# Weight blocks of 128 columns at a pitch of 528 bytes instead of 512 in a partition, in a two-layer decoder kernel

## The reference

```python
def swiglu(h, wg, wu, wd):
    return (jax.nn.silu(h @ wg) * (h @ wu)) @ wd
...
for layer in range(DEPTH):
    h = rms_norm(x, ffn_norm[layer, 0])
    x = x + 0.5 * swiglu(h, ffn_w_gate[layer, 0], ffn_w_up[layer, 0], ffn_w_down[layer, 0])
    h = rms_norm(x, mix_norm[layer])
    if layer % 2 == 0:
        x = x + hybrid_mixer(h, ...)   # attention with three branches, and a short convolution
    else:
        x = x + pool_mixer(h, ...)     # means over windows of 2, 4, 8, 16 tokens, then 256x256 matrices
    h = rms_norm(x, ffn_norm[layer, 1])
    x = x + 0.5 * swiglu(h, ffn_w_gate[layer, 1], ffn_w_up[layer, 1], ffn_w_down[layer, 1])
```

## Time and profile before

| | |
|---|---|
| time of the runs | 1798.89 us median of 3 (1797.44 to 1799.77) |
| the profiled execution | 1798.12 us, of which the span from first to last instruction is 1796.3 us |
| PE busy | 1775.5 us, 99% of the span |
| DVE, ACT, POOL busy | 859.3, 598.6, 92.5 us |
| TensorE clock granted | 1.000 of full speed over the whole span |
| DMA | 163.68 MB, 91 GB/s over the span |
| share of PE in the chain that ended last | 95% |

### The profile page before, as it was taken

How to read it: one execution, slowest core, us unless ns; L and a number is a source line. 1 busy time by engine, 2 the same in 40 slices (tenths; PEclk the granted TensorE clock), 3 DMA queues, 4 the chain that set the end, 5 groups by cost and what they waited for, 6 DMA issues and landing times.

```text
span 1796.3 us, 22196 instructions
## 1 busy us (share of the span) xinstructions
PE 1775.5 (99%) x8164; PEld 1465.8 (82%) x8164; DVE 859.3 (48%) x1104; ACT 598.6 (33%) x838; POOL 92.5 (5%) x81
## 2 busy tenths in 40 slices
PE   8999999999999999999999999999999999999999
PEld 6888888877777878888888888888888888888887
DVE  5544443356788845444443344444432564444322
ACT  5333332235336534333222233232222533332211
POOL 0500000012000011000000000000000000000000
PEclk9999999999999999999999999999999999999999
DMA  6333343324320013333343323333432233333331
GB/s 177 94 93 99 99 115 97 89 75 104 83 82 13 1 47 94 96 102 93 93 125 96 95 82 94 102 96 93 124 97 66 77 94 98 101 93 107 113 96 47
DMA packets 321362, 163.68 MB, mean 91 GB/s; under 512 B 13893, under 2 KB 320041, under 8 KB 321322
## 3 DMA queue, kind: packets, MB, share of 16 engines
q1 hardware_dynamic: 321130, 163.08, 31.5%
q10 hardware_dynamic: 192, 0.08, 0.0%
HBM read 161.04 MB, written 2.10 MB: 91 GB/s over the span
## 4 chain that ended last, share of the span: by engine, by line
PE 95%; DVE 3%; ACT 1%; issue 1%; DMA 0%; SPq 0%; POOL 0%; ACTq 0%; DVEq 0%
PE ps_s L532 20%; PE ps_s L534 20%; PE ps_s L533 20%; PE ps_y L532 9%; PE ps_y L533 9%; PE ps_y L534 9%; PE ps_aux L867 2%; PE ps_y L850 1%; DVE w_lo L1407 1%; PE ps_s L818 1%; PE ps_aux L864 1%; ACT w_hi L1019 1%; PE ps_s L819 0%; PE ps_aux L869 0%; DMA x_in<-in_x 0%
## 5 line engine op out<-in xcount | busy, mean ns | idle before, releaser
L1407 DVE TENSOR_TENSOR w_lo<-raw,w_hi 128x1024 fp32r<-128x1024 f32 (+2 forms) x279 | 368.0, 1319 | 726.4 <-ACT w_hi L1019 725.9
L532 PE MATMUL ps_s<-xg_hi,w_hi 128*128 128x512 f32 x1576 | 618.8, 393 | 0.1
L534 PE MATMUL ps_s<-xg_hi,w_lo 128*128 128x512 f32 x1576 | 613.3, 389 | 0.0
L533 PE MATMUL ps_s<-xg_lo,w_hi 128*128 128x512 f32 x1576 | 613.3, 389 | 0.0
L1019 ACT CAST w_hi<-raw 128x1024 fp32r<-128x1024 f32 (+2 forms) x279 | 312.1, 1119 | 591.9 <-PE ps_s L534 298.1
L532 PEld LDWEIGHTS ps_s<-xg_hi,w_hi 128*128 128x128 f32 x1576 | 295.8, 188 | 65.8 <-issue 2.9
L533 PEld LDWEIGHTS ps_s<-xg_lo,w_hi 128*128 128x128 f32 x1576 | 295.9, 188 | 63.5 <-issue 2.4
L534 PEld LDWEIGHTS ps_s<-xg_hi,w_lo 128*128 128x128 f32 x1576 | 295.8, 188 | 61.9
L532 PE MATMUL ps_y<-act_hi,w_hi 128*128 128x512 f32 x704 | 274.3, 390 | 0.7 <-DVE w_lo L1407 0.7
L534 PE MATMUL ps_y<-act_hi,w_lo 128*128 128x512 f32 x704 | 273.9, 389 | 0.0
L533 PE MATMUL ps_y<-act_lo,w_hi 128*128 128x512 f32 x704 | 273.9, 389 | 0.0
(11 more groups left out here) (314 smaller groups left out, 1078.5 us busy)
## 6 DMA issues: line engine op xcount, KB each, us to landing
raw<-in_ffn_w_gate SPq DMA_DIRECT2D x88, 512.0 KB, 3.9
raw<-in_ffn_w_up SPq DMA_DIRECT2D x88, 512.0 KB, 3.9
raw<-in_ffn_w_down SPq DMA_DIRECT2D x64, 704.0 KB, 4.5
raw<-in_hyb_w_in SPq DMA_DIRECT2D x19, 512.0 KB, 3.8
x_in<-in_x SPq DMA_DIRECT2D x8, 256.0 KB, 6.0
raw<-in_hyb_cmp_w SPq DMA_DIRECT2D x4, 512.0 KB, 4.0
raw<-in_hyb_w_in SPq DMA_DIRECT2D x8, 256.0 KB, 3.3
raw<-in_hyb_w_out SPq DMA_DIRECT2D x16, 128.0 KB, 2.8
```

What stands on the lines that cost most here:

```text
L532: mm(bank, hi, x_hi, start=first, stop=False, **kw)
L533: mm(bank, hi, x_lo, start=False, stop=False, **kw)
L534: return mm(bank, lo, x_hi, start=False, stop=last, **kw)
L1407: tt(w_lo[:, n % 2, 0:size], raw[:, n % 4, 0:size], f32(w_hi[:, n % 2, 0:size]), ALU.subtract).then_inc(lo_ready, 1)
```

## The change

Both weight tensors get a fourth dimension. A block of 128 columns (512 bytes) is followed by 4 unused columns (16 bytes), so blocks stand 528 bytes apart; a slot of 11 blocks grows from 5632 to 5808 bytes, and each tensor by 352 bytes. `w_hi` keeps its position and `w_lo` moves by 352 bytes. The tensors behind `w_lo`, up to `token`, move by 704 bytes; `token` shrinks by 192 bytes (its unused part), so that everything behind it (`act_hi` and all later ones) moves by 512 bytes. `raw` keeps its layout. The cast of ACT and the subtraction of DVE cover the same elements with one more dimension in their access patterns. The order and the number of instructions on every engine are as before.

```diff
@@
 TE = T + 16
 PW = 2 * TE
+WP = P + 4
@@
         raw = sb("raw", [P, 4, KH2 * P])
-        w_hi = sb("w_hi", [P, 2, KH2 * P], F32R)
-        w_lo = sb("w_lo", [P, 2, KH2 * P], F32R)
+        w_hi = sb("w_hi", [P, 2, KH2, WP], F32R)
+        w_lo = sb("w_lo", [P, 2, KH2, WP], F32R)
@@
-        token = sb("token", [P, 80])
+        token = sb("token", [P, 32])
@@
+        def raw_blocks(n):
+
+            return raw[:, n % 4, 0:BLOCKS[n] * P].rearrange("p (k f) -> p k f", f=P)
@@
-                    last_mm = three(bank, w_hi[:, n % 2, k * P:(k + 1) * P], w_lo[:, n % 2, k * P:(k + 1) * P],
+                    last_mm = three(bank, w_hi[:, n % 2, k, 0:P], w_lo[:, n % 2, k, 0:P],
                                     tile_of(x_hi, k0 + k), tile_of(x_lo, k0 + k),
                                     first and k == 0, last and k == BLOCKS[n] - 1)
@@
-                w_h, w_l = (w[:, n % 2, k * 2 * P:(k + 1) * 2 * P] for w in (w_hi, w_lo))
+                w_h, w_l = (w[:, n % 2, 2 * k:2 * k + 2, 0:P] for w in (w_hi, w_lo))
@@
-                copy(w_hi[:, n % 2, 0:BLOCKS[n] * P], raw[:, n % 4, 0:BLOCKS[n] * P]).then_inc(hi_ready, 1)
+                copy(w_hi[:, n % 2, 0:BLOCKS[n], 0:P], raw_blocks(n)).then_inc(hi_ready, 1)
@@
-                size = BLOCKS[n] * P
-                tt(w_lo[:, n % 2, 0:size], raw[:, n % 4, 0:size], f32(w_hi[:, n % 2, 0:size]),
+                size = BLOCKS[n]
+                tt(w_lo[:, n % 2, 0:size, 0:P], raw_blocks(n), f32(w_hi[:, n % 2, 0:size, 0:P]),
                    ALU.subtract).then_inc(lo_ready, 1)
```

More of the change, by code:

```diff
@@ L554, in first_unit @@
                             turn_x(q, (KD - 1,))
-                    hi, lo = (w[:, 0, k * P:(k + 1) * P] for w in (w_hi, w_lo))
+                    hi, lo = (w[:, 0, k, 0:P] for w in (w_hi, w_lo))
                     pe.wait_ge(xg_hi_ready, place + 1)
@@ L613, in block_of @@
                 def block_of(m, k):
-                    return three(ps_s[:, 2 * m, :], w_hi[:, (n + m) % 2, k * P:(k + 1) * P],
-                                 w_lo[:, (n + m) % 2, k * P:(k + 1) * P], tile_of(xg_hi, k), tile_of(xg_lo, k), k == 0, k == KD - 1)
+                    return three(ps_s[:, 2 * m, :], w_hi[:, (n + m) % 2, k, 0:P],
+                                 w_lo[:, (n + m) % 2, k, 0:P], tile_of(xg_hi, k), tile_of(xg_lo, k), k == 0, k == KD - 1)
                 for k in range(KD // 2):
@@ L737, in compress @@
                         last_mm = three(ps_s[:, p % 4, 0:8 * NCP],
-                                        w_hi[:, n % 2, k * P:(k + 1) * P], w_lo[:, n % 2, k * P:(k + 1) * P],
+                                        w_hi[:, n % 2, k, 0:P], w_lo[:, n % 2, k, 0:P],
                                         b_hi, b_lo, h == 0 and k == 0, h == 1 and k == KD - 1)
@@ L907, in from_conv @@
                 for k in range(4, KD):
-                    three(ps_s[:, 2 + d % 2, :], w_hi[:, n % 2, k * P:(k + 1) * P], w_lo[:, n % 2, k * P:(k + 1) * P],
+                    three(ps_s[:, 2 + d % 2, :], w_hi[:, n % 2, k, 0:P], w_lo[:, n % 2, k, 0:P],
                           tile_of(ob_hi, k - 4), tile_of(ob_lo, k - 4), k == 4, False)
@@ L913, in from_attention @@
                 for k in range(4):
-                    last_mm = three(ps_s[:, 2 + d % 2, :], w_hi[:, n % 2, k * P:(k + 1) * P],
-                                    w_lo[:, n % 2, k * P:(k + 1) * P],
+                    last_mm = three(ps_s[:, 2 + d % 2, :], w_hi[:, n % 2, k, 0:P],
+                                    w_lo[:, n % 2, k, 0:P],
                                     tile_of(o_hi, k), tile_of(o_lo, k), False, k == 3)
```

## The result

The changed kernel takes 1830.64 us (median of 4 runs, 1830.29 to 1831.51) against 1798.62 us for the kernel before (also 4 runs), a ratio of 1.018 with a 95% interval of 1.0164 to 1.0196. Its profiled execution has a span of 1829.7 us, 33.4 more than before.

A forecast was written before the change was run, and what follows sets the result against it. The prediction took PE's matmul pace to bound the kernel. Offsets added +36 us, all other terms 0, which on the median of 1798.89 us gave 1835 us, with an 8 in 10 range of 1762 to 1848 us.

The forecast's parts named there:

- part 1: All 6840 matmuls with xg and act: new weight offsets lose the settled 226.7 ns pace for 232.0, +36 us.
- The upper bound, 233.3 ns for all: All 6840 matmuls run at the pace of the matmuls with o, +46 us.
- part 2: Some 190 256-column matmuls, 1.3 us either way, and 96 output-projection matmuls with o, already slow; taken as 0.
- part 3: ACT's cast and DVE's subtraction with one more dimension: at least nothing, at most a start per block; taken as 0.
- The upper bound of 1.4 us more: In DVE's subtraction, seven more starts of 203 ns each, one per block, 1.4 us; as much assumed for ACT.
- The helping rival: Spreading weight blocks removes a collision with the moving tile, so matmuls speed up: between 1753 and 1795 us, chance 0.29.
- The rival of no change: The matmul surcharge hangs on the moving tile's position, or 16 bytes don't matter: 1799 us, chance 0.12.

The follow-up runs named there:

- const64: Kernel before the change with all weight blocks at the pitch of 512 bytes but moved together by 64 bytes; 1841.77 us, ratio 1.0241.
- const16: Kernel before the change with all weight blocks at the pitch of 512 bytes but moved together by 16 bytes; 1840.79 us, ratio 1.0237.
- The map: Matmul-only kernels of their own, writing zeros: weight blocks at constant, then jumping offsets to the tile; constant offset 0 gave 226.6 ns, 32 gave 233.1.
- lo_only: Kernel before the change with the pitch of 528 bytes in w_lo alone, w_hi at 512 and offset 0; 1816.09 us, ratio 1.01.
- aligned: Kernel before the change with gaps bringing ones_r, o_hi, o_lo and pt_b to offset 0 modulo 256 too; 1797.72 us, ratio 0.9999.
- const240: Kernel before the change with all weight blocks at pitch 512, moved to offset 240 modulo 256 from the tiles; 1799.91 us, ratio 1.0011.

## Why the prediction was right

**The bound.** PE's pace was the only thing that moved: 33.1 us more of busy PE in 33.4 us more of span.

**Offsets, part 1.** The term was +36 us, by 232.0 - 226.7 = 5.3 ns on 6840 matmuls. Measured: 231.5 and 232.0 ns, 33.9 us by the starts, 32.0 by the medians. The pace borrowed from the ten matmuls of the earlier trace rows fits the changed kernel to half a nanosecond. The 4 us by which the term is too high are no more than the rounding of its rows: a row is rounded to 0.01 us, so ten matmuls give the pace only to 1 ns. The next use of `ones_r` in the trace of the kernel before has the same ten:

```profile
1055.48 0.39 PE L545 MATMUL ps_stat<-ss_parts,ones_r 128*128 128x512 f32 x1
...
1057.79 0.39 PE L534 MATMUL ps_s<-xg_hi,w_lo 128*128 128x512 f32 x1
```

These are 231.0 ns each, and the unrounded starts give 231.1 to 231.2 in all three places without a stop, which would have made the term 31 us and the time 1830. That the number fits so closely is in part luck in either case. The earlier trace rows average two matmuls at offset 96 and eight that recover at offset 0, while the changed kernel walks over offsets that, held constant, cost between 0 and 7.5 ns. The upper bound, 233.3 ns for all, is what `const64` and `const16` reach at 1841.8 and 1840.8 us: a constant bad offset is worse than the walk, since the walk passes the good ones too.

What I gave as the reason needs mending in two places. I said that the fast pace was seen only where the offset stays at 0 from one load to the next. The map shows a period of 256 bytes and further offsets that hold the fast pace, and bring it back after some stretches and not after others. And the jump is not what hurts. A pitch of 768 jumps by 256 bytes with every block and stays at 226.7. What counts is that loads stand at a bad offset modulo 256, even one in three of them (`lo_only`), and what ran before.

**256-column matmuls and `o`, part 2.** Taken as 0. In the changed kernel `o` lost some of its surcharge (233.3 before, 230.0 to 233.6 after), on 96 matmuls under 0.3 us. The pool mixer's stretch of the earlier trace rows went from 119.6 to 118.2 ns by the unrounded starts, and the compression's last two from 118.0 and 118.7 to 122.7; each comes to under 0.3 us.

**ACT and DVE, part 3.** Taken as 0; 1049 and 1243 ns measured. The extra dimension costs 5 ns on DVE and nothing on ACT. The upper bound of 1.4 us more is far off.

**The helping rival** fell: no constant offset of 32, no low block elsewhere and no pitch was faster than 226.6 ns. The compression's 113.2 ns, which spoke for it, did not carry over to tiles of 512. Its own two stretches do get slower at offset 0 (`aligned`), so for those 256-column matmuls an offset other than 0 is the faster one; whether that comes from the short run read four times no run shows. **The rival of no change** falls with `const16` and `const64`, in which only the weights stand elsewhere (all other tensors keep their places modulo 512). With it goes the price of 0 that the prediction drew from the page "SBUF — State Buffer" of the Trainium skill, section "Who interferes with whom": there PE has two independent read ports and never waits on anyone, while here the same matmuls take 226.7 or 233.3 ns each by position. In the maps no other engine works meanwhile, so what they show is not contention between engines.

What stays open is the mechanism. That weight load and moving read meet in the same part of the memory would fit a dependence on the difference alone, but no run looks inside. What carries the memory of the pace from one stretch to the next is not shown either.

## What to carry to other kernels

Where PE is the bound and its matmuls run back to back, read the distance of two starts and compare it with columns divided by the clock. Of what is left the layout of SBUF set up to 6.7 ns here; 13.3 ns stayed in the best layout that was tried. For fp32r matmuls of 512 columns keep stationary and moving operand at the same position modulo 256 bytes, and look at a stretch where another operand is used before moving anything: two such stretches forecast this change to within some 4 us. Take the pace from many starts, since the rows are rounded. A pad of 16 bytes between blocks cost 1.8% here.

## What the runs showed that was not expected

- The surcharge of an fp32r matmul of 512 columns has a period of 256 bytes in the difference of the positions of its operands: 226.7 ns at 0, about 233 at most others, 228.9 at 192.
- It has a memory: at a difference of 16 bytes the pace is 233.6 ns after a stretch at 32 and 226.8 after one at 0, and the slow one lasted for over a thousand matmuls in `const16`. After a slow stretch at 80 it was fast at once.
- At 240 there are two paces as well, 228.6 and 226.8, and one whole FFN of `const240` ran at the slower while the others ran at the faster.
- After a short stop of PE some six matmuls were at 229 to 235 ns too, though all offsets are 0 (`aligned`, at 381.75 us).
